# Six of twelve convolution-branch projections as three Strassen pairs

## The reference

```
h = rmsnorm(x)
a_b, a_c, a_x, qb, kb, vb, qc, kc, vc, qi, ki, wi, g_a, g_b, g_c = split(h @ w_in)
br_a = (a_b * causal_dwconv(a_c * a_x, conv_a)) @ w_a_out      # a_b, a_c, a_x: 512 wide each
br_b = sliding-window attention(qb, kb, vb) @ w_swa_o          # 8 heads of 64, window 128
br_c = attention over keys picked by an indexer(qi, ki, wi)    # top 256 of up to 1024
merged = sigmoid(g_a) * br_a + sigmoid(g_b) * br_b + sigmoid(g_c) * br_c
x = x + merged @ w_out;  x = x + convolutional gated FFN(rmsnorm(x))
```

## Time and profile before

| | us |
|---|---|
| median of 3 runs | 1763.06 (1762.79 to 1763.23) |
| the profiled execution | 1763.54 |
| its span | 1761.7 |
| TensorE busy | 1728.5 (98%) |
| VectorE busy | 1290.3 (73%) |
| ScalarE busy | 735.3 (42%) |
| GpSimd busy | 545.7 (31%) |

### The profile page before, as it was taken

One profiled execution on the slowest core, in us unless ns is written; L12 is line 12 of the kernel. 1 busy time (PEld: TensorE's weight loads), 2 busy tenths in 40 slices (PEclk: granted clock), 3 DMA queues, 4 the chain that ended last, 5 costly groups with the idle time before them and its releaser, 6 DMA issues.

```text
span 1761.7 us, 31930 instructions
## 1 busy us (share of the span) xinstructions
PE 1728.5 (98%) x12179; PEld 1689.5 (96%) x12179; DVE 1290.3 (73%) x2159; ACT 735.3 (42%) x1293; POOL 545.7 (31%) x441
## 2 busy tenths in 40 slices
PE   6999999999999999999999999999999999999998
PEld 6999999999999999888899999999999999999998
DVE  6367889958797876687758989766666665875765
ACT  5342112368812233777644554333333333422334
POOL 2211212257745431000021102555555554121130
PEclk9999999999999999999999999999999999999999
DMA  4111111110244414522324111222222223533212
GB/s 156 49 26 53 37 34 48 45 41 25 55 139 129 143 39 132 163 88 77 112 83 156 49 49 49 85 86 77 82 74 80 78 86 97 178 116 108 65 37 99
DMA packets 179189, 146.41 MB, mean 83 GB/s; under 512 B 10140, under 2 KB 149676, under 8 KB 179052
## 3 DMA queue, kind: packets, MB, share of 16 engines
q1 hardware_dynamic: 178076, 142.54, 26.0%
q0 software_dynamic: 976, 2.00, 0.4%
HBM read 118.22 MB, written 26.28 MB: 82 GB/s over the span
## 4 chain that ended last, share of the span: by engine, by line
PE 91%; DVE 4%; ACT 2%; issue 1%; DMA 1%; POOL 1%; SPq 0%; DVEq 0%; ACTq 0%; POOLq 0%
PE ps L1480 34%; PE ps L1911 23%; PE ps L1984 7%; PE ps L1970 7%; PE ps L1627 4%; PE ps L1607 4%; PE ps L1492 4%; PE ps L1841 3%; PE ps L1753 3%; PE ps L1701 1%; PE ps L1708 1%; PE ps L1510 1%; DMA x_rows<-in_x_prompt 0%; DVE probs L3091 0%; PE ps L1713 0%
## 5 line engine op out<-in xcount | busy, mean ns | idle before, releaser
L1480 PE MATMUL ps<-h_hi,w_hi 128*128 128x352 f32 (+1 forms) x912 | 199.5, 327 | 0.0
L1480 PE MATMUL ps<-h_hi,w_lo 128*128 128x352 f32 (+1 forms) x912 | 196.5, 323 | 0.0
L1480 PE MATMUL ps<-h_lo,w_hi 128*128 128x352 f32 (+1 forms) x912 | 196.2, 323 | 0.0
L1201 POOL TENSOR_TENSOR w_lo<-w_raw,w_hi 128x1024 fp32r<-128x1024 f32 (+1 forms) x51 | 96.1, 1884 | 322.0 <-ACT w_hi L2072 322.0
L2885 DVE MAX8 top<-key_mask 128x8 f32<-128x512 f32 (+5 forms) x176 | 161.6, 920 | 10.9 <-DVE key_mask L2885 1.9
L2885 DVE MATCH_REPLACE8 key_mask<-top,key_mask 128x512 f32<-128x512 f32 (+5 forms) x176 | 159.0, 907 | 0.3 <-issue 0.3
L1480 PEld LDWEIGHTS ps<-h_hi,w_lo 128*128 128x128 f32 (+1 forms) x912 | 155.5, 186 | 0.5
L1480 PEld LDWEIGHTS ps<-h_hi,w_hi 128*128 128x128 f32 (+1 forms) x912 | 153.3, 187 | 2.6 <-issue 0.9
L1480 PEld LDWEIGHTS ps<-h_lo,w_hi 128*128 128x128 f32 (+1 forms) x912 | 154.2, 186 | 0.5
L1911 PE MATMUL ps<-mix_hi,quarter_hi 128*128 128x264 f32 x672 | 136.9, 285 | 0.3 <-ACT x_one L2072 0.3
L1911 PE MATMUL ps<-mix_hi,quarter_lo 128*128 128x264 f32 x672 | 136.4, 284 | 0.0
(11 more groups left out here) (409 smaller groups left out, 4625.1 us busy)
## 6 DMA issues: line engine op xcount, KB each, us to landing
w_raw<-in_w_in SPq DMA_DIRECT2D x54, 256.0 KB, 3.1
w_hi<-gate_highs SPq DMA_DIRECT2D x48, 256.0 KB, 2.8
w_lo<-gate_lows SPq DMA_DIRECT2D x48, 256.0 KB, 3.0
ffn_tiles<-t SPq DMA_DIRECT2D x44, 264.0 KB, 2.4
w_raw<-in_w_gate SPq DMA_DIRECT2D x44, 256.0 KB, 3.1
w_raw<-in_w_up SPq DMA_DIRECT2D x44, 256.0 KB, 3.1
w_raw_in_lo<-in_w_in SPq DMA_DIRECT2D x30, 256.0 KB, 3.0
w_raw<-in_w_down SPq DMA_DIRECT2D x32, 192.0 KB, 2.7
```

The lines of the kernel that those rows point to most:

```text
L1201: nc.gpsimd.tensor_tensor(WLO[:, k, 0:tiles, :], raw[:, k, 0:tiles, :], WHI[:, k, 0:tiles, :].bitcast(F32), ALU.subtract).then_inc(lo_read ...
L1480: last = nc.tensor.matmul(PS[0:rows, NB * k + b, 0:e - a], w[:, k, t, 0:rows], x[:, t, a:e], start=m == 0 and w is WHI and x is hi, stop=m ...
```

## The change

The first six projections of the branch (tiles 0 and 1 complete) stay as they are (`A_WHOLE`). The last six become three pairs of seven products: (a_b of tile 2, a_b of tile 3), (a_c, a_x of tile 2), (a_c, a_x of tile 3).

- SyncE loads each pair's two 512 KB weights into the one buffer `RAW`, as its quarters come free (`free_quarters`).
- GpSimd makes 4 weight sums and 7 low parts of 512 columns a pair; before, it made one low part of 1024 columns a projection. The 1.29 us kind of operation thus replaces the 2.4 us kind. The store of the indexer's key rows stands behind the first sum.
- ScalarE makes 7 high parts and 5 copies out of PSUM a pair, and the high parts of the mixes.
- VectorE makes four mixes of h once, 2112 columns each: 1 and 2 in the indexer's projections, 4 and part of 3 during the sixth whole projection, the rest behind its `conv_input`, with low parts; the convolution of tile 1 stands behind them. Then come 3 additions a pair, the inputs and the convolutions of tiles 2 and 3.
- Selection rounds of `SEL[3]`: 11 in the branch instead of 26; 7 in the window attention, one at y = 2, 4 to 14; 8 in the gate loop, one a pass. Its `to_mask` moves behind the gate loop. Six stay where they were.

```diff
-J_GA = J_A + 3 * CT
+A_WHOLE = 6
+J_GA = J_A + A_WHOLE
+A_PAIRS = ((C_AB + 2 * P, C_AB + 3 * P), (C_AC + 2 * P, C_AX + 2 * P), (C_AC + 3 * P, C_AX + 3 * P))
+A_SLOTS = [n % 4 for n in range(NQ * len(A_PAIRS) - 1)] + [2]
+A_SUMS = (Q_S1, Q_S2, Q_S4, Q_S3)
+MIXES = (1, 2, 4, 3)
...
-        SELECTS_A = {5: 5, 6: 1, 7: 5, 8: 5, 9: 1, 10: 5, 11: 4}
+        LATE_ROUNDS = range(2, 16, 2)
+        A_TILES = [(B2, B3), (T1, T3), (T0, T1)]
+        A_RAW = (T1, T1, B2, T1)
...
SyncE:
+            def free_quarters(p, half):
+                if p == 0:
+                    free(J_GA, 0, half)
+                else:
+                    sp.wait_ge(sums_ready, 4 * p)
+                    sp.wait_ge(q_lo_ready, NQ * (p - 1) + DOWN_ORDER.index(Q_A22 if half else Q_A12) + 1)
...
GpSimd (a_weight_sum: one addition or subtraction of two quarters; a_low: quarter minus its high part):
+            for p in range(len(A_PAIRS)):
+                n = NQ * p
+                a_low(n)
+                a_weight_sum(p, Q_S1)
+                if p == 0:
                     pool.wait_ge(rows_out, R_IDX_K + 3)
...
+                a_weight_sum(p, Q_S2)
+                a_low(n + 1)
+                a_weight_sum(p, Q_S4)
+                a_low(n + 2)
+                a_low(n + 3)
+                a_weight_sum(p, Q_S3)
+                for m in range(4, NQ):
+                    a_low(n + m)
...
TensorE:
-            for m in range(3 * CT):
+            for m in range(A_WHOLE):
...
+            def a_product(p, q, hi, lo, tile=0, at=0, first=False):
+                n, bank = NQ * p + DOWN_ORDER.index(q), a_bank(p, q)
+                pe.wait_ge(q_lo_ready, n + 1)
+                for t in range(KH):
+                    for w, x in ((WHI, hi), (WHI, lo), (WLO, hi)):
+                        for b in range(2):
+                            last = nc.tensor.matmul(
+                                PS[:, 2 * bank + b, 0:QP], a_slot(w, n)[:, t, :],
+                                x[:, tile + t, at + b * QP:at + (b + 1) * QP],
...
+                a_product(p, Q_A11, H_HI, H_LO, first=True)
+                if p == 0:
+                    pe.wait_ge(taken[1], evicted(J_GA - 1))
+                else:
+                    pe.wait_ge(a_added, landed(done_before + 1))
+                a_product(p, Q_S1, *mixed(1), first=True)
+                pe.wait_ge(a_copied, copied + 1)
+                a_product(p, Q_S2, *mixed(2))
+                pe.wait_ge(a_copied, copied + 2)
+                a_product(p, Q_S4, H_HI, H_LO, tile=KH, at=HALF)
+                pe.wait_ge(a_copied, copied + 3)
+                a_product(p, Q_S3, *mixed(3))
...
+                a_product(p, Q_A12, H_HI, H_LO, tile=KH, first=True)
+                pe.wait_ge(a_copied, copied + 4)
+                a_product(p, Q_A22, *mixed(4))
...
ScalarE, behind the copies of the whole projections (a_weight_high: high part of a quarter or sum;
hmix_high: of a mix; a_block: one copy of 528 columns out of PSUM):
+            for n in range(1, 4):
+                a_weight_high(n)
+            hmix_high(4)
+            for n in range(NQ * len(A_PAIRS)):
+                p, q = n // NQ, DOWN_ORDER[n % NQ]
+                act.wait_ge(product_done, n + 1)
+                if q not in (Q_S4, Q_A12):
+                    a_block(p, q)
+                if n == 1:
+                    hmix_high(3)
+                if n == NQ - 2:
+                    a_high(1)
+                if n + 4 < NQ * len(A_PAIRS):
+                    a_weight_high(n + 4)
...
VectorE (hmix: two or three steps of 2112 columns; hmix_lower: the low part; a_conv: states,
convolution, product with the gate; a_lower: low part of a tile):
+                hmix(1 if n == 1 else 2)
+                if n == 2:
+                    hmix_lower(1)
...
+            for m in range(A_WHOLE):
...
-                if m in SELECTS_A:
-                    select((SEL[3], SELECTS_A[m]))
+                if m == A_WHOLE - 1:
+                    hmix(4)
+                    hmix_lower(2)
+                    hmix(3, (0,))
...
                 conv_input(k, T1)
                 dve.wait_ge(taken[k], J_A // 2 + i + k)
...
+                if m == A_WHOLE - 1:
+                    hmix(3, (1, 2))
+                    hmix_lower(4)
+                    hmix_lower(3)
+                a_conv(t, T0)
+                a_lower(t)
...
+                def add(to, other, q, copies):
+                    if p == 1 or p == 2 and q != Q_S4:
+                        select((SEL[3], 6 if q == Q_S4 else 1))
+                    dve.wait_ge(product_done, NQ * p + DOWN_ORDER.index(q) + 1)
+                    dve.wait_ge(a_copied, landed(5 * p + copies))
+                    V_.tensor_tensor(halves(to), other, halves(to), ALU.add).then_inc(a_added, 1)
...
+            a_adds_of(0)
+            a_adds_of(1)
+            select((SEL[3], 1))
+            a_input(1)
+            a_conv(2, B2)
+            a_adds_of(2)
+            a_lower(2)
+            a_input(2)
+            a_conv(3, B3)
+            a_lower(3)
...
+                    if window and y in LATE_ROUNDS:
+                        select((SEL[3], 1))
...
+            gates(J_GB, ((SEL[4], 2), (SEL[2], 1), (SEL[1], 1)), ((SEL[4], 2), (SEL[2], 1), (SEL[3], 1)))
             to_mask(SEL[3])
-            gates(J_GB, ((SEL[4], 2), (SEL[2], 1), (SEL[1], 1)), ((SEL[4], 2), (SEL[2], 1)))
+            dve.wait_ge(masks_out, 2)
             to_mask(SEL[4])
```

More of the change, by code:

```diff
@@ L2820, in _, with block, hmix, hmix_lower @@
             step.wait()
+            def block(buf, key, late):
+                return buf[:, KH * key:KH * (key + 1), HALF * late:HALF * (late + 1)].bitcast(F32)
+            MIXED = {1: ((0, 1), (0, 0)), 2: ((1, 1), 1), 4: ((1, 0), 2), 3: ((0, 1), (1, 1))}
+            def hmix(d, steps=(0, 1, 2)):
+                to, (first, second) = MIX_RAW[d][:, :, :], MIXED[d]
+                whole = isinstance(second, int)
+                work = [(block(H_HI, *first), MIX_RAW[second][:, :, :] if whole else block(H_HI, *second), ALU.subtract),
+                        (to, block(H_LO, *first), ALU.add)]
+                if not whole:
+                    work.append((to, block(H_LO, *second), ALU.subtract))
+                for m in steps:
+                    if m >= len(work):
+                        continue
+                    x, y, op = work[m]
+                    last = V_.tensor_tensor(to, x, y, op)
+                    if m == len(work) - 1:
+                        last.then_inc(hmix_raw, 1)
+                        dve.wait_ge(hmix_raw, landed(MIXES.index(d) + 1))
+                    else:
+                        step.mark(last)
+                        step.wait()
+            def hmix_lower(d):
+                dve.wait_ge(hmix_hi, landed(MIXES.index(d) + 1))
+                V_.tensor_tensor(MIX_LO[d][:, :, :], MIX_RAW[d][:, :, :], MIX_HI[d][:, :, :].bitcast(F32),
+                                 ALU.subtract).then_inc(hmix_low, 1)
             for n in range(1, J_A):
@@ new lines, in _, with a_input @@
+                a_conv(t, T0)
+                a_lower(t)
+            def a_input(p):
+                first, second = A_TILES[p]
+                dve.wait_ge(a_copied, landed(5 * p + 5))
+                dve.wait_ge(a_added, landed(a_adds(p) + 3))
+                V_.tensor_tensor(U[:, 2:2 + SEQ], first[:, 0:SEQ], second[:, 0:SEQ], ALU.mult)
+                last = V_.tensor_tensor(U[:, SEQ + 4:TOK + 4], first[:, SEQ:TOK], second[:, SEQ:TOK], ALU.mult)
+                if p == 1:
+                    last.then_inc(a_added, 1)
+                    dve.wait_ge(a_added, landed(a_adds(2)))
+                else:
+                    step.mark(last)
+                    step.wait()
```

172 lines of the change are left out of this document (147 added, 25 removed).

## The result

The changed kernel takes 1774.8 us (median of 6, 1771.25 to 1775.23) against 1763.08 (median of 6, 1762.70 to 1763.49): ratio 1.0061, 95% interval 1.0048 to 1.0074. It is slower by 11.7 us, beyond the forecast of 1767.4 and its range. The profiled execution took 1771.67 us, 8.1 more than that of before; it is one of the two quickest of the six, the other four lie at 1774.6 to 1775.2. Both parts need explaining.

A forecast was written before the change was run, and what follows sets the result against it. TensorE, busy 98% of the span, was taken to bound the kernel. The terms -8.5 (matmuls), +7.7 (late pairs) and +5.1 (window attention) sum to +4.3: 1767.4 us in the median, range 1757.5 to 1771.5.

The forecast's parts named there:

- Matmuls, -8.5: Pair stage on TensorE: 432 matmuls of 352 columns (70.0 us) replaced by 504 of 264 (61.5), gaining 8.5 us.
- The first pair, +7.6: Pair stage: VectorE and GpSimd taking turns, plus queue order, start the second pair's S1 at 31.0, 7.6 us late.
- The later pairs, +0.1: Second and third pair, without mixes: they stay in step within 0.5 us, costing 0.1.
- The window attention, +5.1: Seven selection rounds moved there exceed VectorE's idle time by 6.7, less 1.6 of slack: 5.1 us.
- Rival C: Pair stage: the later pairs are late too, by one product's 2.9 us; 1770.4, chance 0.18.
- The slack of 1.6: Window attention: mask step done at 405.99, matmul came at 407.57; a slack of 1.6 us, used up once.
- the 6.7 by which VectorE was counted over: Window attention: rounds of 2.19 us against VectorE's idle time per step, over by 6.7 us in sum.
- The gate loop and the early mixes, 0: Eight rounds and the mask conversion in the gate loop, and mixes 1 and 2 in the index projections, cost 0.
- -0.8: Pair stage in all: -8.5 for matmuls + 7.7 for lateness of the pairs = -0.8 us.
- Rival A: Pair stage: turns do not order these large operations, so the stage loses only 1.3; 1761.0, chance 0.16.
- B: Window attention takes its seven rounds for nothing; 1762.3, chance 0.18.

The follow-up runs named there:

- fourth experiment: Changed kernel with two steps of mix 3 and low parts of mixes 4 and 3 replaced by MAX8 reading one SBUF input; 1765.32 us, ratio 1.0016.
- sixth kernel: Changed kernel with one of the two late steps of mix 3 moved ahead of the sixth projection's convolution input; 1767.31 us, ratio 1.0028.
- first profile: The changed kernel itself, profiled in the first measurement; that execution took 1771.67 us, one of the two quickest of six.
- third experiment: Kernel before, all projections whole, with only the selection rounds and the mask placed as in the changed kernel; 1769.37 us, ratio 1.0038.
- second experiment: Changed kernel with its seven window-attention rounds elsewhere: four ahead of the last query low parts, two at y = 29 and 31, one behind; 1768.84 us.
- seventh: Changed kernel with three edits: window-attention rounds relocated, ScalarE's order of mix high parts changed, one mix 3 step earlier; 1764.59 us, ratio 1.0010.
- eighth: The seventh with the third pair's two selection rounds moved behind the last convolution tile; 1769.36 us, ratio 1.0037.
- ninth: The seventh with two rounds behind mix 3's last step, then low parts of mixes 3 and 4, S4's addition, then tile 1's convolution; 1761.60 us.
- tenth: The ninth with the third pair's two rounds behind the window attention, three there instead of one; 1764.76 us, ratio 1.0011.
- eleventh: The ninth with the first pair's addition of S3 ahead of tile 1's low part, and the round behind the window attention at y = 32; 1760.22 us.
- first experiment: The changed kernel again, no edit; 1774.60 us, ratio 1.0071; its profiled run, the changed kernel's second profile, took 1773.04 us.

## Why the prediction was wrong

The direction was right, and so were both places; the size was 4.3 against 11.7. The profiled execution has 8.1 of the 11.7. By the prediction's own terms:

- **Matmuls, -8.5**: right. The FFN's and the gate loop's runs keep their rates, and products of the stage that wait for nothing take 2.90 to 2.94 us. In the stage TensorE is busy 64.88 us, of which 61.5 are the products and 1.7 the lower clock. The other 1.6 sits at the starts of products: where operands come just in time, the first two matmuls take 0.48 to 0.52 us instead of 0.41, and eight products without a listed wait take 2.99 to 3.08. The fourth experiment has the same 1.6 (63.12).
- **The first pair, +7.6**: this step failed. The second pair's S1 starts at 33.2, not 31.0, and the order of events was another. S1 did start on time, since the convolution input reads PSUM and takes no turn; GpSimd got its low part of S1 out before the first step of the mix. S2 did stand the 3.5 us that were forecast, but by luck: it waited for GpSimd's low part (start at 9.6, not 11.4) and not for ScalarE's copy of A11. I had given GpSimd one turn between two VectorE operations of 2.4 each; in fact it needs 3.4 for each of three. S3 started at 19.6, not 17.5, since mix 3's high part is queued behind the copy of S1; I had it behind that of A11. With it the low part, convolution tile 1 and the addition that S1 wants are late.
- **The clock had no price**. The prediction read a clock of 1.00 in rows where TensorE never stood. The Trainium skill says that it can matter ("TensorE: Matmul & The Clock Gate", section "HAM oscillation — how this bites in real kernels": gaps of TensorE bring the throttle back), and the trace agrees: 0.92, then 0.73 behind 3.54 us of idle time. But in the first pair of the changed kernel it costs nothing: with S2 taking 3.2, 4.7 or 5.6 us, S4 starts 5.64 to 5.66 behind S2. It costs 1.7 where nothing hides it, as at the end of the sixth kernel's third pair.
- **The later pairs, +0.1**: in the first profile 0.7 more, the slow product starts from the second pair's S1 on. In the median this step failed. The third pair's last addition was played to be 0.4 us early. Its margin hangs on who takes the turn at 222 us; the first profile won it and the second lost it, for 2.2 us, and the clock can fall on top (1.7, seen in the sixth kernel). Rival C named the margin, at +2.9 and a chance of 0.18; that it is what most runs of the changed kernel do is argued, not shown.
- **The window attention, +5.1**: mis-sized, 6.8. The slack of 1.6 should not have been subtracted: it was read at one mask and one matmul, and one pair of rows does not show that the whole queue is ahead by it. That the 6.7 by which VectorE was counted over comes so near is in part luck: in between the delay grew by 8.1 and 1.3 of it came back. The third experiment gives 6.6 for the rounds alone, the second 5.8 back with 1.4 lost in the gate loop.
- **The gate loop and the early mixes, 0**: right here (+0.1 and 0). But the later experiments show how close the loop was. With one selection round of VectorE between the window attention and it, TensorE waits 1.3 to 1.4 at its end (second, seventh, eighth and ninth), with three 2.6 (tenth), with none nothing (fourth and eleventh).

Together, in the profile: -0.8 became +2.1 in the stage (2.2 in the first pair, 0.7 behind it), +5.1 became +6.8, the gate loop 0.1, and 0.9 came back at the end: 8.1. The remaining 3.6 of the median's 11.7 would be the third pair's stall of 2.2 with a fall of the clock in most runs; that part is not shown. Rival A (no turns at this size) and B (rounds for nothing) are refuted by the fourth and the third experiment.

## What to carry to other kernels

Replacing a VectorE operation that reads one SBUF input by one that reads two is not neutral, even at the same length: look at what GpSimd has in that stretch, and put the operations that don't take turns (here the selection rounds, and reads of PSUM) beside GpSimd's urgent ones. Work that has no deadline still needs idle time of its engine in a stretch where nobody waits for it; count idle time per step, and don't subtract a slack read at one row. When margins of a few tenths decide, forecast both outcomes as groups and compare medians group against group. Price a stall of TensorE with the clock that it can lose, but only where no later wait hides the loss: behind the same stall of 3.5 us a product took 3.2, 4.7 or 5.6 us here, and the next one started at the same time.

## What was not expected of the hardware

Between 30 and 1650 us the granted clock fell to its lower level, 1.2 GHz, behind stalls of TensorE alone, but not behind each. Behind stalls of 3.1, 3.5, 3.6 and 4.1 us it fell in every profile but one (the second experiment's, where it stayed at 1.00 behind 3.54 and fell behind the next wait, of 2.49); it fell behind one of 2.6, and behind one of 2.2 in one profile and not in another; behind stalls of 1.3 to 1.7 us it stayed at 1.00. A fall took 1.4 to 1.7 us from TensorE's work, in the first experiment's profile 2.4 (S2 took 5.6 us instead of 3.2). Beside an operation of 2112 columns on VectorE a 128x512 one on GpSimd took 3.40 us instead of 1.29, and the VectorE one 3.38 instead of 2.36; beside MAX8 of the same 2112 columns both kept their own price (2.38 and 1.28).
